# Up products of the feed-forward networks issued two at a time, with their TensorE passes going to two PSUM banks by turns

## What is computed

```python
def conv_ffn(x, w_up, conv_w, conv_b, w_down):            # twice; FFN_DIM = 3072
    u = causal_depthwise_conv(x @ w_up, conv_w, conv_b)   # three taps over time
    g, val = jnp.split(u, [FFN_DIM], axis=-1)
    return (jax.nn.gelu(g) * val) @ w_down

def hybrid_layer(...):                                    # twice; D_FF = 4096
    ...
    hf = rms_norm_2(x, g_ffn)
    x = x + jnp.square(jax.nn.relu(hf @ w_up)) @ w_down
```

## Time and profile before

| what | us |
|---|---|
| median of 3 runs | 2792.51 (2792.32 to 2792.86) |
| the profiled execution, its own time | 2792.07 |
| the profiled execution, first to last instruction (span) | 2790.3 |
| PE busy / DVE / ACT / POOL | 2772.5 / 1245.8 / 1241.7 / 1225.5 |
| granted TensorE clock, mean | 0.998 of full speed |

### The profile page before, as it was taken

How to read it: one execution, slowest core, us unless ns; L and a number is a source line. 1 busy time by engine, 2 the same in 40 slices (tenths; PEclk the granted TensorE clock), 3 DMA queues, 4 the chain that set the end, 5 groups by cost and what they waited for, 6 DMA issues and landing times.

```text
span 2790.3 us, 32430 instructions
## 1 busy us (share of the span) xinstructions
PE 2772.5 (99%) x12950; PEld 2261.4 (81%) x12950; DVE 1245.8 (45%) x2087; ACT 1241.7 (45%) x1813; POOL 1225.5 (44%) x545
## 2 busy tenths in 40 slices
PE   9999999999999999999999999999999999999998
PEld 8876888888888888887777888888877778888887
DVE  4676551544675435327666432021266674420112
ACT  4665442444864334334774343143246744442331
POOL 3222444444554444443555444444434564444443
PEclk9999999999999999999999999999999999999999
DMA  4222332333233323332222323333322223233332
GB/s 153 91 69 62 97 100 90 105 99 93 89 98 102 100 91 100 98 98 84 69 76 84 106 91 98 98 98 97 100 91 77 68 84 98 91 98 99 98 98 76
DMA packets 74726, 259.25 MB, mean 93 GB/s; under 512 B 9856, under 2 KB 9856, under 8 KB 74576
## 3 DMA queue, kind: packets, MB, share of 16 engines
q1 hardware_dynamic: 73280, 255.08, 29.3%
q10 hardware_dynamic: 1296, 2.10, 0.2%
HBM read 254.95 MB, written 2.13 MB: 92 GB/s over the span
## 4 chain that ended last, share of the span: by engine, by line
PE 96%; DVE 2%; ACT 1%; DMA 0%; issue 0%; POOL 0%; SPq 0%; DVEq 0%; ACTq 0%
PE ps L463 28%; PE ps L465 28%; PE ps L464 28%; PE ps L539 2%; PE ps L570 2%; PE ps L553 1%; PE ps L596 1%; PE ps L598 1%; PE ps L597 1%; PE ps L474 1%; PE ps L519 1%; PE ps L521 1%; PE ps L520 1%; ACT pbuf L1023 0%; ACT w_hi L963 0%
## 5 line engine op out<-in xcount | busy, mean ns | idle before, releaser
L2074 POOL TENSOR_TENSOR w_lo<-raw,w_hi 128x1024 fp32r<-128x1024 f32 x469 | 1130.6, 2413 | 1482.8 <-ACT w_hi L963 1482.6
L463 PE MATMUL ps<-xs,w_hi 128*128 128x512 f32 x2176 | 861.7, 396 | 1.6 <-DVE xs L1464 1.6
L465 PE MATMUL ps<-xs,w_lo 128*128 128x512 f32 x2176 | 847.1, 389 | 0.0
L464 PE MATMUL ps<-xs,w_hi 128*128 128x512 f32 x2176 | 847.0, 389 | 0.0
L963 ACT ACTIVATE w_hi<-raw 128x1024 fp32r<-128x1024 f32 x470 | 494.6, 1054 | 637.6 <-PE ps L465 601.2
L463 PE MATMUL ps<-hid,w_hi 128*128 128x512 f32 x1316 | 514.5, 391 | 0.0
L465 PE MATMUL ps<-hid,w_lo 128*128 128x512 f32 x1316 | 512.2, 389 | 0.0
L464 PE MATMUL ps<-hid,w_hi 128*128 128x512 f32 x1316 | 512.1, 389 | 0.0
L463 PEld LDWEIGHTS ps<-xs,w_hi 128*128 128x128 f32 x2176 | 408.5, 188 | 96.2 <-issue 8.3
L464 PEld LDWEIGHTS ps<-xs,w_hi 128*128 128x128 f32 x2176 | 408.6, 188 | 88.6 <-issue 5.2
L465 PEld LDWEIGHTS ps<-xs,w_lo 128*128 128x128 f32 x2176 | 408.5, 188 | 85.5
(11 more groups left out here) (234 smaller groups left out, 2571.6 us busy)
## 6 DMA issues: line engine op xcount, KB each, us to landing
raw<-in_weights SPq DMA_DIRECT2D x470, 512.0 KB, 3.5
btab<-in_rel SPq DMA_DIRECT2D x8, 256.0 KB, 4.1
out<-tmp ACTq DMA_DIRECT2D x8, 256.0 KB, 2.0
hT<-in_x SPq DMA_DIRECT2D x3, 512.0 KB, 7.0
btab<-in_heads SPq DMA_DIRECT2D x6, 256.0 KB, 4.0
tmp<-in_heads SPq DMA_DIRECT2D x6, 256.0 KB, 3.9
common<-in_fixed SPq DMA_DIRECT2D x1, 642.0 KB, 10.3
hT<-in_x SPq DMA_DIRECT2D x2, 256.0 KB, 4.0
```

The source lines that it names most:

```text
L463: pe.matmul(banks[bank][:], wh, rh, start=(k == 0), stop=False)
L464: pe.matmul(banks[bank][:], wh, rl, start=False, stop=False)
L465: last = pe.matmul(banks[bank][:], wl, rh, start=False, stop=(k == len(specs) - 1))
L2074: gp.tensor_tensor(w_lo[:, n % NPAIR, :], raw[:, n % NRAW, :], w_hi[:, n % NPAIR, :].bitcast(F32), ALU.subtract).then_inc(*w_low.tick(n))
```

## The change

A new function `linear_pair` does two up products at once. For each chunk k it puts the blocks of both products into the weight order one after the other, waits for the later of their slabs, and then issues six passes: high by high into bank A, high by high into bank B, high by low into A, high by low into B, low by high into A, low by high into B. In the networks of the first block the two products are the gate half and the value half of a step; in those of the second block they are blocks c and c + 1. A slab so holds four chunks of both products, where it held eight chunks of one. Both slabs are opened under the group of the first product. The first network's `square_sum` runs between the chunks of the pair, and `root` is issued after the pair. The code of ACT, DVE, POOL and SP is the same text as before.

```diff
-            def linear(bank, group, specs, rhs, operand, k0=0, k1=None, between=None):
+            def linear(bank, group, specs, rhs, operand, k0=0, k1=None):
...
+            def linear_pair(two_banks, groups, specs, rhs, operand, between=None):
+
+                for k in range(len(rhs)):
+                    parts = []
+                    for group, own in zip(groups, specs):
+                        key = (group, k)
+                        if key not in place:
+                            put(key, P, own[k], (groups[0], 0))
+                        slab, at = place[key]
+                        parts.append((slab, w_hi[:, slab % NPAIR, at:at + P], w_lo[:, slab % NPAIR, at:at + P]))
+                    rh, rl = rhs[k]
+                    T.wait_ge(w_low, max(slab for slab, wh, wl in parts))
+                    operand(k)
+                    if k == 0:
+                        for bank in two_banks:
+                            wait_bank(bank)
+                    for bank, (slab, wh, wl) in zip(two_banks, parts):
+                        pe.matmul(banks[bank][:], wh, rh, start=(k == 0), stop=False)
+                    for bank, (slab, wh, wl) in zip(two_banks, parts):
+                        pe.matmul(banks[bank][:], wh, rl, start=False, stop=False)
+                    for group, bank, (slab, wh, wl) in zip(groups, two_banks, parts):
+                        last = pe.matmul(banks[bank][:], wl, rh, start=False, stop=(k == len(rhs) - 1))
+                        done = ([group] if k == len(rhs) - 1 else []) + ([("slab", slab)] if (group, k) in closes else [])
+                        if done:
+                            last.then_inc(*product.tick(*done))
+                    if between:
+                        between(k)
...
                     for c in range(12 * part, 12 * part + 12):
+                        two = (2 * c % 6, 2 * c % 6 + 1)
+                        linear_pair(two, [("up", L, c, half) for half in range(2)],
+                                    [mat("ffn_w_up", L, P * (c + 24 * half)) for half in range(2)], xr, x_chunk(m),
+                                    between=square_sum if c == 0 and m == 1 else None)
                         for half in range(2):
-                            bank = (2 * c + half) % 6
-                            first = c == 0 and half == 0
-                            linear(bank, ("up", L, c, half), mat("ffn_w_up", L, P * (c + 24 * half)), xr, x_chunk(m),
-                                   between=square_sum if first and m == 1 else None)
-                            free[bank] = (taps, ("up", L, c, half))
-                            if first and m != 1:
-                                root(m)
+                            free[two[half]] = (taps, ("up", L, c, half))
+                        if c == 0 and m != 1:
+                            root(m)
...
-                    for c in range(16 * part, 16 * part + 16):
-                        bank = c % 6
-                        linear(bank, ("up2", L, c), mat("w_up_2", L, P * c), xr, x_chunk(5 + 2 * L))
-                        free[bank] = (scaled, ("up2", L, c))
+                    for c in range(16 * part, 16 * part + 16, 2):
+                        two = (c % 6, c % 6 + 1)
+                        linear_pair(two, [("up2", L, c), ("up2", L, c + 1)],
+                                    [mat("w_up_2", L, P * c), mat("w_up_2", L, P * c + P)], xr, x_chunk(5 + 2 * L))
+                        for i in range(2):
+                            free[two[i]] = (scaled, ("up2", L, c + i))
```

## The result

The changed kernel takes 2818.59 us (median of 4 runs, 2817.9 to 2820.36) against 2792.41 us: a ratio of 1.0095, 95% interval 1.0083 to 1.0107. That is 26.2 us slower; 19.2 us were forecast. The profiled execution has a span of 2817.4 us, 27.1 more than before.

A forecast was written before the change was run, and what follows sets the result against it. TensorE's gapless stream of passes was taken to bound the kernel. 4.6 + 9.9 + 3.6 + 0.8 + 1.6 - 1.3 = +19.2 us gave 2811.7 us, range 2802 to 2822 (own range 2807 to 2817, chance 0.62).

The forecast's parts named there:

- 1 steady gaps: First-block networks: late slabs at every second pair and at first down products, 22 x 0.21 = 4.6 us.
- 2 two large gaps: Both first-block networks' starts: norm after the pair makes slab n+4 late by 4.94 us each, 9.9 us.
- 3 last hidden chunk, four times: First-block down products: chunk 11 waits 0.90 us for the last step's low part, four times, 3.6 us.
- 4 behind the softplus: After part 0 of the first network: ACT's softplus before the copy makes slab n+4 late, 0.8 us.
- 5 bank 0 in the second block: Second block: first down product wants bank 0, used by the last pair, at once; 0.8 us twice, 1.6 us.
- 6 start of the first network: First network: 0.3 of the single 1.6 us wait stays as each chunk feeds six passes, -1.3 us.
- rival of the longer chain: First-block pairs: a DVE operation stretched under POOL's low part adds 0.4 per gap, 9 us more, 2820; chance 0.15.
- rival of the banks: Up products: alternating banks shortens 3840 passes, at most 51 us, to 2760; 2770 at the skill page's figure; chance 0.07.
- only the starts count: First-block networks: the steady chain just fits and the last-hidden-chunk waits halve, 2805 us; chance 0.12.
- no change: Whole kernel: ACT and POOL keep up and the starts are absorbed, so the time stays; chance 0.04.

The follow-up runs named there:

- the mended pair: Changed kernel with order A, A, A, B, B, B, ACT's copies of slabs n+4 and first network's n+1 sooner, second block's banks shifted in part 1: 2792.12 us.
- the slabs alone: Changed kernel's slabs and late norm product kept, but 24 passes of the first product run, then 24 of the second: 2809.15 us.
- the copy ahead of the chain: Changed kernel, but in first-block networks ACT copies slab n+4 before the norm's square root and the first taps: 2802.14 us.
- three passes in a row: Changed kernel with a chunk's six passes ordered A, A, A, B, B, B instead of by turns: 2809.38 us.
- the norm at half of the pair: Changed kernel with the norm's product issued after chunk 3 of the first pair in networks two to four: 2813.04 us.
- the one with the copy sooner: Kernel before, but in the first network's approach ACT copies slab n+1 ahead of its square of chunk 3: 2790.31 us.

## Why the prediction was right, and where it was short

The direction, the mechanism and the places held: of the 27.1 us of span, item by item (from the starts of the same passes in both timelines; TensorE also enters the first network 0.2 us sooner than before, 263.01 against 263.23):

| item | forecast | measured |
|---|---|---|
| 1 steady gaps | 4.6 | 6.0 |
| 2 two large gaps | 9.9 | 10.0 |
| slow passes behind them | none | 3.6 |
| 3 last hidden chunk, four times | 3.6 | 2.9 |
| 4 behind the softplus | 0.8 | 0.8 |
| 5 bank 0 in the second block | 1.6 | 1.8 |
| 6 start of the first network | -1.3 | +2.0 |

The measured 2818.59 us lies in the range of 2802 to 2822, but outside 2807 to 2817, where the forecast put its chance of 0.62. It is nearest to the 2820 of the rival of the longer chain, and that is not what happened. The wide range reached that far for the sake of that rival. So part of the hit is luck: nothing in the prediction stood for the slow passes or for the loss at the start, and the misses of the items add up to 8.6 us one way and 0.7 the other.

The items are sums of durations along one engine's order, and 2, 4 and 5 came out within 0.2 us. Item 3 is 0.7 smaller, since the down product itself starts late by a steady gap, which item 1 counts. ACT's order was the cause, not a slow engine: when only that order changed, 16.5 us went; when only the norm moved, 5.6. Item 1 is 1.4 larger: most gaps are the 0.2 forecast, those at the third pair of each part 1 are 0.5, and the passes behind a gap take some ns more.

**The step that was mis-sized is item 2:** it priced a gap by its length alone. Each gap left TensorE at 1.2 GHz for 8 to 11 passes, 0.2 us each beyond their usual time, 3.6 us together. Filling the gaps took 3.8 off. The Trainium skill, "TensorE: Matmul & The Clock Gate", section "What's actually happening", says that being throttled is the default and activity lifts it. These traces agree: behind the idle time the granted clock is 0.50, the passes are back at their usual distance after those 8 to 11, and with the gap filled the clock stays at 1.00.

**Item 6 has the wrong sign.** Its step was "each chunk now feeds six passes", with the wait on the chunk as the only one. It looked at the activations and not at the weights. The second slab is wanted 24 passes in, before and after. But before, these were the passes of all eight chunks of x, with their sums of squares and the wait between, and the second product began at 277.05; now they are those of four chunks of both products, and TensorE stands at chunk 4 at about 271.2. In the first network that slab's low part was only ready at 273.05. The wait of 1.6 us on DVE did go, and one of 1.9 us on POOL took its place, with slow passes behind it in the profiled execution: of the 2.0 us some 1.6 are those, and 0.4 are left without them, where -1.3 was forecast. With the copy issued sooner, the mended pair has neither wait.

The rival of the banks is refuted by equal counts of passes in equal windows. The longer chain, by DVE under POOL's low part, did not occur in the pairs of the first block; in the third network one such operation took 2.45 us (1688.42, under POOL's at 1685.56), and no pass came later for it. That only the starts count is refuted by the 6.0 us of steady gaps, and no change by the time itself. The prediction did not tell apart what comes from both halves ending at once and what from the slabs; the slabs alone show that items 1 and 3 come from the first, and the late slab at the first network's start from the second. Item 2 can't be put down to one edit: it takes the norm issued later and the copy behind the chain, and either mended alone takes it away where it was mended.

What stays open: why the clock fell behind the 1.9 us of idle time at the first network's start in some executions and not in others. Five traces have this wait. In 4.5 us from 274 the granted clock is 0.62 in the changed kernel and with the copy ahead of the chain, and 1.00 with three passes in a row, with the norm at half of the pair and with the gap filled. Four of these five kernels issue the same passes up to there, so the edits do not explain it. It is worth 1.6 us, of the 2.5 us by which the runs of the changed kernel differ, and a span of a single execution can be off by as much. The row of the copy ahead of the chain:

```profile
274.00:278.50 4.50, 4.50 (x11) 2.89 (x12) 1.62 (x3) 0.46 (x1) 0.00 (x0) 0.62 0.40 117
```

Also open is why the steady gap at the third pair of each part 1 is 0.5 us and not 0.2.

## What to carry to other kernels

Where TensorE runs without a gap, joining two products changes only when their results come, and lumps them: look at which in-order engine has to work through both before it issues the next load, and at the slab that is wanted first. Issuing that copy in front of the chain took 16.5 of the 26.2 us back here by itself; the rest needed a bank that is free in time, the first slab copied sooner and an earlier end of the first half, and 1.8 us stayed against a kernel before with the same early copy. Price a gap of TensorE by its length and by the passes behind it at the lower clock.

## What was not expected of the hardware

A wait of 4.6 us put the next 8 to 11 passes at 427 ns instead of 226.7 (granted clock 0.50), and one of 2.9 us, with the slabs alone, about seven. One of 1.9 us slowed passes in two traces (0.62 over 4.5 us) and did not in three others (1.00). Twenty useless passes in each of two gaps made a kernel 3.8 us faster. And DVE operations on SBUF operands were stretched from 0.75 us to between 2.33 and 2.38 us when they met a low part of POOL, in the kernel before, the changed one and the one with the copy sooner.
